# A four-layer trunk with seven-product MLPs: another order in the first round of each MLP, and weight sums made by adding DMA transfers in the other rounds

## The reference, cut to what matters

```
x = x + mixer(rmsnorm(x, norm_mix[i]))
x = x + squared_relu_mlp(rmsnorm(x, norm_mlp[i]), mlp_w1[i], mlp_w2[i])

def _rmsnorm(x, g):  y = x * rsqrt(mean(x * x) + 1e-6);  return y * g
def _squared_relu_mlp(h, w1, w2):
    return jnp.square(jax.nn.relu(h @ w1)) @ w2      # w1 1024 x 4096, w2 4096 x 1024
```

## Time and profile before

| | us |
|---|---|
| median of 3 runs | 2027.25 (2026.68 to 2027.87) |
| the profiled execution's own time | 2027.66 |
| its span in the trace | 2025.8 |
| PE busy | 2000.3 (99%) |
| DVE busy | 1432.3 (71%) |
| ACT busy | 1063.8 (53%) |
| POOL busy | 247.3 (12%) |
| DMA moved | 193.20 MB, mean 95 GB/s |

### The profile page before, as it was taken

The page is one execution under the profiler, slowest core; times in us unless marked ns, Lnnn a source line. Parts: engine busy times, 40 slices in busy tenths (PEclk is TensorE's granted clock), DMA queues, the critical chain, the costliest instruction groups (busy, mean ns, idle before and its releaser), DMA issues.

```text
span 2025.8 us, 28746 instructions
## 1 busy us (share of the span) xinstructions
PE 2000.3 (99%) x11760; PEld 1748.8 (86%) x11760; DVE 1432.3 (71%) x1682; ACT 1063.8 (53%) x1508; POOL 247.3 (12%) x323
## 2 busy tenths in 40 slices
PE   9999999999999999999999999999999999999998
PEld 8888898989878789899888888898988888899897
DVE  7866865756897867567698786675787758667574
ACT  6655534625466646254456663553647646353453
POOL 7002000000200200002731200000641011000000
PEclk9999999999999999999999999999999999999999
DMA  6222324314223133241332242422422223242431
GB/s 193 61 68 78 120 64 125 113 57 143 86 81 103 64 125 115 61 148 57 119 89 70 61 138 84 125 84 83 148 76 71 59 67 122 66 146 63 125 115 42
DMA packets 152595, 193.20 MB, mean 95 GB/s; under 512 B 17712, under 2 KB 95088, under 8 KB 152464
## 3 DMA queue, kind: packets, MB, share of 16 engines
q1 hardware_dynamic: 145520, 186.04, 29.6%
q0 software_dynamic: 4544, 3.94, 0.7%
q10 hardware_dynamic: 2400, 1.38, 0.2%
HBM read 185.30 MB, written 2.10 MB: 93 GB/s over the span
## 4 chain that ended last, share of the span: by engine, by line
PE 89%; DVE 6%; POOL 2%; ACT 2%; DMA 1%; issue 1%; ACTq 0%; DVEq 0%; POOLq 0%; SPq 0%
PE psum L674 27%; PE psum L676 27%; PE psum L675 27%; DVE h_lo L1514 2%; PE psum L1113 2%; PE psum L1086 1%; DVE w_lo L1479 1%; DMA arena<-in_mlp_w 1%; PE psum L1221 1%; DVE arena_r L1675 1%; PE psum L1062 1%; PE psum L1058 1%; PE psum L1057 1%; PE psum L1063 0%; DVE arena L1611 0%
## 5 line engine op out<-in xcount | busy, mean ns | idle before, releaser
L1479 DVE TENSOR_TENSOR w_lo<-w_raw,w_hi 128x1024 fp32r<-128x1024 f32 (+1 forms) x303 | 374.5, 1240 | 239.5 <-ACT w_hi L2400 238.3
L2400 ACT ACTIVATE w_hi<-w_raw 128x1024 fp32r<-128x1024 f32 (+1 forms) x307 | 323.6, 1060 | 328.3 <-PE psum L676 292.7
L674 PE MATMUL psum<-u_hi,w_hi 128*128 128x512 f32 x1256 | 492.2, 392 | 0.1
L676 PE MATMUL psum<-u_hi,w_lo 128*128 128x512 f32 x1256 | 489.1, 389 | 0.0
L675 PE MATMUL psum<-u_lo,w_hi 128*128 128x512 f32 x1256 | 489.1, 389 | 0.0
L674 PE MATMUL psum<-h_hi,w_hi 128*128 128x256 f32 (+1 forms) x1368 | 440.4, 322 | 0.0
L675 PE MATMUL psum<-h_lo,w_hi 128*128 128x256 f32 (+1 forms) x1368 | 437.5, 320 | 0.0
L676 PE MATMUL psum<-h_hi,w_lo 128*128 128x256 f32 (+1 forms) x1368 | 437.3, 320 | 0.0
L676 PEld LDWEIGHTS psum<-u_hi,w_lo 128*128 128x128 f32 x1256 | 235.8, 188 | 49.6
L674 PEld LDWEIGHTS psum<-u_hi,w_hi 128*128 128x128 f32 x1256 | 235.9, 188 | 49.0 <-DVE u_lo L1809 1.2
L674 PEld LDWEIGHTS psum<-h_hi,w_hi 128*128 128x128 f32 x1368 | 260.3, 190 | 20.2 <-issue 1.1
(11 more groups left out here) (333 smaller groups left out, 2589.3 us busy)
## 6 DMA issues: line engine op xcount, KB each, us to landing
w_raw<-in_mlp_w SPq DMA_DIRECT2D x176, 512.0 KB, 3.9
arena<-in_mlp_w SPq DMA_DIRECT2D x80, 512.0 KB, 4.9
w_raw<-in_mla_w_o SPq DMA_DIRECT2D x16, 512.0 KB, 3.8
w_raw<-in_lru_w_in SPq DMA_DIRECT2D x16, 512.0 KB, 3.9
w_raw<-in_swa_w_in SPq DMA_DIRECT2D x12, 512.0 KB, 4.2
w_raw<-in_mla_w_ukv SPq DMA_DIRECT2D x8, 512.0 KB, 4.7
w_raw<-in_lru_w_out SPq DMA_DIRECT2D x8, 512.0 KB, 3.6
w_raw<-in_swa_w_o SPq DMA_DIRECT2D x8, 512.0 KB, 4.0
```

Of the source, the lines that this page charges most:

```text
L674: nc.tensor.matmul(out, stat[0], mov[0], start=start, stop=False, skip_group_check=skip)
L676: return nc.tensor.matmul(out, stat[1], mov[0], start=False, stop=stop, skip_group_check=skip)
L1479: ins = nc.vector.tensor_tensor(w_lo[:, to], tile, exact(w_hi[:, to]), ALU.subtract)
L2400: nc.scalar.activation(w_hi[:, to], raw_tile(op.raw), ACT.Copy).then_inc(w_hi_done, 1)
```

## The change

Three things are edited.

1. *First rounds, buffers.* The second half (q = 1) of the ordinary group's result no longer goes to the `relu` buffer but to `b12`, which has been used up by then.
2. *First rounds, order.* They get a program of their own, `first_round`, on ACT and on DVE. The norm's sums are split earlier (`sums_hi`, `sums_lo`). The root, the variance and the whole of q = 1 go behind the copies of `c11`, `c21` and `c22`. Two raw sums are made later. On PE only a wait changes: the first `down` group asks for the parts of `u` one at a time.
3. *The other 24 rounds, weight sums.* A round loads five raw blocks, not four. Two of them get a second block of `w1` added by a DMA that POOL issues (`accum_op=ALU.add`); DVE makes two sums, not four. ACT waits for such a block on `second_added`. The loads get other slots.

```
+        a, e, b = (Raw(block(half, n), phase, True) for half, n in ((0, 0), (1, HALF), (1, 0)))
+        p = Raw(block(0, 0), phase, True, plus=block(0, HALF))
+        q = Raw(block(0, HALF), phase, True, plus=block(1, HALF))
+        raws.extend((a, p, q, e, b))
+        ops.append(Operand("A11", a))
+        a.freed = len(ops)
+        ops.append(Operand("A11+A21", p, (p, e)))
+        ops.append(Operand("A11+A21+A22", p, made=sums + 1))
+        ops.append(Operand("A12", b, (b, p)))
+        ops.append(Operand("A21+A22", q))
...
+        ops.append(Operand("A11+A12+A21+A22", b, made=sums + 2))
...
+            def units_of_first_u(kp):
+                pe.wait_ge(u_ready, c.now("u_ready") + (1, 2, 4, 4)[kp])
...  (DVE)
+            def add_blocks(to, other):
+                dve.wait_ge(w_loaded[other.slot], other.landed)
+                nc.vector.tensor_tensor(raw_tile(to), raw_tile(to), raw_tile(other), ALU.add).then_inc(sums_made, 1)
...
+            def first_round(r):
+                c.add("rounds")
+                c.add("tensor_unit", 3)
+                split(2)
+                nc.vector.tensor_tensor(b21, b21, b11, ALU.add).then_inc(turned_made, 1)
+                split(1)
+                turned_lo(T4, b21)
+                product_passed()
+                dve.wait_ge(c_copied, 3 * r + 1)
+                nc.vector.tensor_tensor(c11, bank(2, 1), c11, ALU.add).then_inc(c_added, 1)
+                split(1)
...
+                root_ready()
+                norm_var()
...
+                squares_of(1)
+                split(1)
+                low_of_squares(1)
...  (ACT)
-                norm_root(bank(3, 1))
-                c.add("psum_done")
-                split(1)
-                high_of_squares(1)
                 c.add("u_ready", 2)
...
+            def first_round(r):
+                c.add("rounds")
+                product_passed()
+                act.wait_ge(u_ready, c.now("u_ready") - 1)
+                nc.scalar.activation(c11, bank(2, 0), ACT.Copy).then_inc(c_copied, 1)
+                split(2)
...  (POOL)
+            def second_blocks(start, end):
+                for raw in raws[start:end]:
+                    if raw.plus is not None:
+                        pool.wait_ge(w_loaded[raw.slot], raw.landed)
+                        src = source(raw.plus)
+                        g.dma_start(raw_tile(raw).rearrange("p (a n) -> p a n", n=src.shape[2]), src,
+                                    accum_op=ALU.add).then_inc(second_added[raw.slot], 16)
```

More of the change, by code:

```diff
@@ L136, with __init__ @@
 class Raw:
-    def __init__(self, unit, phase, extra=False):
-        self.unit, self.phase, self.extra = unit, phase, extra
+    def __init__(self, unit, phase, extra=False, plus=None):
+        self.unit, self.phase, self.extra, self.plus = unit, phase, extra, plus
         self.freed = None
 class Operand:
-    def __init__(self, role, raw, others=(), made=None):
-        self.role, self.raw, self.others, self.made = role, raw, others, made
+    def __init__(self, role, raw, adds=(), made=None):
+        self.role, self.raw, self.adds, self.made = role, raw, adds, made
 def weight_plan():
-    raws, ops, raw_starts = [], [], []
+    raws, ops, raw_starts, late = [], [], [], []
     sums = 0
@@ L234, in weight_plan @@
         landed[raw.slot] += 16 * LOADS.get(raw.unit[0], 1)
+        added[raw.slot] += 16 * (raw.plus is not None)
+        raw.added = added[raw.slot]
         raw.landed = landed[raw.slot]
-    return raws, ops, raw_starts
+    return raws, ops, raw_starts, late
 EXTRA = 2
@@ L1719, in seven_products @@
                 c.add(f"area{xy}")
+            def first_round(r):
[10 more added lines that the diff above has]
+                product_passed()
+                dve.wait_ge(c_copied, 3 * r + 3)
+                nc.vector.tensor_tensor(c22, c22, bank(2, 0), ALU.subtract).then_inc(c_added, 1)
+                root_ready()
+                norm_var()
+                c.add("psum_done")
+                product_passed()
+                free(nc.vector.tensor_tensor(c21, bank(3, 0), c21, ALU.subtract), 3)
+                squares_of(1)
+                split(1)
+                low_of_squares(1)
+                split(1)
+                u_lo_of(1, 0)
+                split(1)
+                c.add("tensor_unit")
+                split(1)
+                c.add("area2")
             def mlp(gain):
@@ L1747, in mlp @@
                         seven_products(0)
-                    seven_products(1)
+                        seven_products(1)
+                    else:
+                        first_round(c.now("rounds"))
                     u_lo_of(1, 1)
@@ L2393, in split @@
                     to = slice(at, at + op.raw.unit[-1])
-                    if op.made is None:
+                    if op.made is not None:
+                        act.wait_ge(sums_made, op.made)
+                    elif op.raw.plus is not None:
+                        act.wait_ge(second_added[op.raw.slot], op.raw.added)
+                    else:
                         act.wait_ge(w_loaded[op.raw.slot], op.raw.landed)
-                    else:
-                        act.wait_ge(sums_made, op.made)
                     need(act, unit_done, c.now("unit") + 1 - SLOTS)
@@ L2528, in seven_products @@
                 split(1)
[L2529 to L2531 removed]
+                if g == 1:
                     u_hi_of(0, 1)
@@ L2553, in seven_products @@
                 c.add("u_ready", 2)
+            def first_round(r):
+                c.add("rounds")
+                product_passed()
+                act.wait_ge(u_ready, c.now("u_ready") - 1)
+                nc.scalar.activation(c11, bank(2, 0), ACT.Copy).then_inc(c_copied, 1)
+                split(2)
+                product_passed()
+                product_passed()
+                nc.scalar.activation(c21, bank(2, 0), ACT.Copy).then_inc(c_copied, 1)
+                split(1)
+                turned_hi(T4, b21)
+                need(act, x_ready, c.now("x_ready"))
+                nc.scalar.activation(c22, bank(3, 0), ACT.Copy).then_inc(c_copied, 1)
+                c.add("tensor_unit", 3)
+                split(1)
+                norm_root(bank(3, 1))
+                c.add("psum_done")
+                act.wait_ge(c_added, 2 * r + 2)
+                link(nc.scalar.activation(c22, c22, ACT.Relu))
+                split(1)
+                high_of_squares(1)
+                act.wait_ge(area_free[3], jobs["round", r][1])
+                split(1)
+                link(nc.scalar.activation(first_tokens, first_tokens, ACT.Relu))
+                act.wait_ge(u_ready, c.now("u_ready"))
+                u_hi_of(1, 0)
+                split(1)
+                product_passed()
+                nc.scalar.activation(c12, bank(2, 0), ACT.Relu).then_inc(area_free[2], 1)
+                split(1)
+                act.wait_ge(area_free[2], jobs["round", r][0])
+                c.add("u_ready", 2)
             def half_gained(n, ks):
```

148 lines of the change are left out of this document (74 added, 74 removed).

## The result

| | before | after |
|---|---|---|
| median (lowest to highest) of 4 runs each, us | 2027.09 (2026.68 to 2027.87) | 2006.32 (2006.04 to 2007.59) |
| profiled execution's own time, and its span | 2027.66, 2025.8 | 2007.59, 2005.8 |

The ratio is 0.9898, 95% interval 0.9881 to 0.9915: 20.8 us less. The forecast was 2007.1. The two profiled executions lie 20.1 us apart (their spans 20.0), since that of the changed kernel is 1.3 above its median; what is read from the traces is to be held against the 20.0.

The account below looks back on a forecast made before the run. PE, busy 99% of the span, was taken to bound the kernel. 2027.66 less 21.4 (11.0 + 5.1 + 4.3 + 1.0) plus 1.2 gave 2007.5, at the median 2007.1 us; range 2004 to 2027.

Parts of the forecast that it names:

- L760's stop: PE's wait for the split sum of squares, once before each first round: to go in full, 4.3 us.
- T1's: PE's one wait at T1 for the copy of `c21`: to go, 1.0 us.
- The stops: PE's waits in and before the first rounds, all to go: `c11` copy 11.0 us, L760 4.3, T1 1.0.
- The clock: Halved clock behind three of the four long `c11` waits, to go with them: 3 x 1.7 = 5.1 us.
- The residual: New PE waits in the reordered first rounds: 0.3 us per MLP, 1.2 in all, bounds 0 and 2.5 each.
- The places to watch: First rounds, spare before PE waits: T4's lo part 0.4 us, sum in `c22` 0.8, last lo part of `u` 0.8.
- The adding transfers: Other 24 rounds: landing taken at 8 us, between 3.9 and 29.6, in time everywhere, cost 0.
- one of my signs of being wrong: Second rounds: ACT's `w_hi` waiting for a DMA was listed among what would show the prediction wrong; no size given.
- 1 (the order moves the wait): First rounds: waits up to 2.5 us each at three tight places, one or two halved clocks; 2010 to 2020 us, chance 0.15.
- 2 (block e late, deciding at a landing of 7.0): Twelve second rounds: block e, asked for one unit later, holds up DVE's sum; at 9 us landing 2031 us, chance 0.10.
- 3 (adding transfer over 14 us): Second rounds of later slices: block q late for PE 12 times; at 16 us landing 2063 us, chance 0.08.
- 4: Waits return in full elsewhere in first rounds, or small losses in the 24 rounds eat the gain; 2023 to 2027, chance 0.07.

Follow-up runs that it names:

- both half-changes: Order only: changed kernel with VectorE making all four weight sums, 2007.09 us. Adding transfers only: changed kernel with the old first rounds, 2027.47 us.
- the last experiment: Changed kernel, first rounds: DVE's first down unit `w_lo` ahead of squares q = 1, ACT's next `w_hi` ahead of q = 1's hi part; 2004.68 us.
- The experiment on DVE alone: Changed kernel with DVE's first down unit `w_lo` ahead of squares q = 1, ACT's order kept; 2007.16 us.
- another run without a delay: Changed kernel with DVE's first down unit `w_lo` ahead of squares q = 1, ACT's order kept; 2007.16 us, its trace from the run of 2008.24.

## Why the prediction was right

**Mechanism.** The order was said to make the gain and the adding transfers to be worth nothing: shown by both half-changes (2007.09 and 2027.47). The copy of `c11` was to end at 213.8 and ended at 214.22, since it waits for q = 0's lo part as worked out. Its spare of 1.0 us was 1.2 in the first MLP, but 0.1, 0.7 and 1.3 in the others: that the wait went in full in the second was luck by 0.1 us. L760's stop and T1's went as predicted.

**The sum, term by term.** It came to 20.2 us off and 20.8 was measured, but three terms were mis-sized and made up for each other: that the two numbers agree to 0.6 us is in part luck.
- *The stops* were taken at their brackets, 11.0 + 4.3 + 1.0 = 16.3 us. From start to start they are more: 3.0 us four times for `c11` (215.51 to 218.57, less the 0.12 of a step, and 0.11 behind it), 5.4 for L760 (1.31 to 1.65 less 0.23 each, and 0.11 behind), 1.3 for T1: 18.7 us.
- *The clock* was taken at 3 x 1.7 = 5.1 from means over 10 us. Part of the low clock lay within the stop, where nothing runs. Before the change the matmuls behind the stop of 218.57 step by 0.21 in place of 0.12 for 13 steps; the first two of them:

```profile
218.95 0.41 PE L675 MATMUL psum<-arena_r,w_hi 128*128 128x256 f32 x1
219.16 0.41 PE L676 MATMUL psum<-arena_r,w_lo 128*128 128x256 f32 x1
```

  That is 1.25 us and 0.15 for the first step: 1.4 each, 4.2 in all.
- *The residual* of 1.2 us is four times 0.52 = 2.1 us by the last experiment, and it lies at a place that the prediction had not listed: the `w_lo` of the first down unit, behind squares q = 1.
- 18.7 + 4.2 - 2.1 = 20.8. Matched matmul by matmul, the two traces give 21.1 us for the four MLPs. Against them stands 1.0 us that the profiled execution lost in its first 15 us, on the `w_lo` of the list of waits; that and a few small differences elsewhere bring it to the 20.0 between the spans. That the sum meets the 20.8 between the medians to the tenth is chance.

**The places to watch.** T4's lo part was to end at 222.9 and did at 223.6, the sum in `c22` at 225.3 and did at 226.0, the last lo part of `u` at 239.0 and did at 239.84: all 0.7 to 0.8 us late. But PE too came 0.7 us later than worked out in this execution, to T2 at 215.48 and not at 214.8. What counts is the spare, and it was right: T4 began at 224.01 (spare 0.4, as predicted), H22 at 226.89 (0.9, for 0.8), the third `down` unit at 241.22, 1.4 behind the lo part, 0.5 of it by the gap of the `w_lo` (0.9 without it, for 0.8). None of them stops PE. The experiment on DVE alone, where that lo part came 1.1 us later against PE, goes past it: PE stopped there for 0.4 us.

**The adding transfers.** I had taken 8 us to landing; it is 7.0 in the median of all, between bounds of 3.9 and 29.6, but 9.6 (8.1 to 11.9) at the twelve places that decide, where by the prediction 9.5 to 12.3 were free before ACT is late. So the term came out near nothing with less to spare than I gave it: three of the twelve were late for ACT, and its lead over PE, which I had put at about 2 us, took up two of them. ACT's `w_hi` waiting for a DMA in the second rounds, one of my signs of being wrong, did come, three times, and cost 0.6 us once. The estimate from the Trainium skill's DMA: Bandwidth & Descriptors (Anatomy of one DMA — SWDGE (gpsimd) path) with the doubled reads of Collectives: The Full Stack was 4.4 us; the trace's lowest is 6.0, so the measurement decides, and that estimate is 1.6 us too low even for the fastest one. An issue costs POOL 1.28 us, not the 0.5 of its small transfers: 62 us in all, not 24, hidden as POOL is 15% busy.

**The rivals.** 1 (the order moves the wait) holds for 2.1 us of its 3 to 13. 2 (block e late, deciding at a landing of 7.0): plain loads landed in 3.9 and 4.7 in the median, block e itself in 4.2 to 6.1 in the twelve rounds, and DVE's raw sum waited for one only 0.3 us; it did not come, and block e was not delayed by itself, so the point at which it decides was not tried. 3 (adding transfer over 14 us): 11.9 was the longest, and 13.3 in another run without a delay. Its price was of the right size: 7.4 us of delay and 6.2 to landing, 13.6 us in all, gave 2032.7, where I had 2063 for 16 us. 4 is ruled out by the time itself and by the list of waits.

## What to carry to other kernels

A stop of PE is priced from start to start around it, against the usual step: its bracket leaves out about 0.27 us, a stop of 0.30 us had no bracket at all, and an "issue" of a few tenths that comes once in every pass can be another engine's instruction that ended 0.1 us before. Ahead of an operand copy that frees a PSUM bank, put nothing that isn't needed before it: here the root and two `w_hi`, 4 us in all, cost up to 14 us in four places. A spare worked out at one of several like places is that place's alone: here four of them had 0.1 to 1.3 us. Work taken off an engine that is not late is worth nothing, but a transfer that takes it over is free only while it lands in time: take its landing at the place that decides, not the median of all, and in a graded delay read the landing again, since a later issue can land faster.

## What the runs showed of the hardware

- An adding transfer of 512 KB from HBM into SBUF, issued by POOL: 1.27 to 1.39 us on POOL, 6.0 / 7.0 / 11.9 us from issue to landing, against 3.9 for a plain load by SP. With no plain load in flight beside it, it took 6.0 to 6.4 us; with four or more, 8.1 to 11.9; the same transfers issued 5.3 us later took 6.0 to 6.5.
- The clock's fall to 1.2 GHz is not decided by the length of the stop alone near 2 us: it followed stops of 2.15, 2.17 and 3.11 us and did not follow ones of 1.72 and, in another MLP, 2.17. In the kernel before it followed three of four stops of 2.7 to 2.8 us. Where I counted, it lasted for 13 and 16 matmuls that step by 0.21 us, and it costs 1.4 to 1.5 us.
